# Identity products ahead of TensorE's waits in three layer norms and in the routing of a two-layer decoder trunk

## The chip, the cores and the metric

The kernel runs on one core of one Trainium2 chip. The metric is the device time of that core in microseconds (us), from one launch to its end. Several launches of the kernel before were timed, and one more was recorded by the hardware profiler.

## The reference

x has 256 tokens of 1024 channels, in float32. Two layers follow each other, each a mixer and a channel mixer, each followed by a residual layer norm:

```
layer 0:  x = LN(alpha*x + deltanet(x));   x = LN(alpha*x + swiglu(x))        # D_FF 2816
layer 1:  k, v = x @ w_kv
          x = LN(alpha*x + sliding_window_attention(x, k, v))
          x = LN(alpha*x + moe(x))                                            # 8 experts, 2 per token
moe(x):   logits = x @ w_router;  top_v, top_i = top_k(logits, 2)
          gates = one-hot sum of softmax(top_v)
          out = sum over e of gates[:, e] * ((silu(x @ g_e) * (x @ u_e)) @ d_e)
```

So there are four layer norms. The first three (after the DeltaNet mixer, after the dense SwiGLU, after the attention) are the inner ones; the last one ends the program and is not touched.

## The kernel before

**Products.** Every large product is made of three float32r products of a high and a low part (hi·hi, hi·lo, lo·hi). Weights arrive in units of 1 MB (two DMAs of 512 KB) in six `raw` slots; ScalarE cuts the high part (`cut_hi`, line 484), VectorE the rest (`cut_lo`, line 790), into three `hi`/`lo` slots. SyncE's queue issues the DMAs; each waits until VectorE has cut the unit that lay in its slot. TensorE waits for `lo_ready` of the unit it needs, uses it, and increments `unit_used`, on which ScalarE's next cut waits. Matmuls of all stages are issued by the helper `mm`, line 1226.

**Order of work.** Each engine has one hand-written program, and semaphores tie them together; nothing is reordered. On TensorE the inner norms look like this: `to_tokens` finishes the projection of the two token blocks of 128, block 0 first. VectorE's `norm` (lines 800 to 823) then works through block 0 and block 1: residual add out of PSUM (line 809), statistics (813, 815, 816), `x - mean` times gain (820), and, when POOL has raised the variance to the power -1/2 (line 374), the last step (823), which sets `ln_done`. TensorE's `turn_x` transposes the normed x in four steps `s` of four 128x128 blocks (line 1237), two steps per token block; before steps 0 and 2 it waits for `ln_done` of the block. ScalarE copies each step out of PSUM (`xT_hi`, line 490), VectorE takes the rest (`xT_lo`, line 798), and the first product of the next stage waits for these (`turn_lo`).

**Routing, after the third inner norm.** TensorE waits for the turned x (`turned_in(4)`), makes the logits by `small_product` (24 matmuls of 256 columns, line 1226), and signals `lg_mm`. VectorE cuts the low part of x for the gather (line 1100) and then copies the logits (line 1102, `lgT_here`); TensorE transposes them (line 1550); VectorE finds the two best experts in a chain of small operations and sets `sel_here` (line 1121); TensorE sums the selection with a triangular and an all-ones matrix (`pos_mm`), VectorE makes the gates, the positions and `cint` (lines 1124 to 1137, `route_here`), and the one-hot matrices (line 1148, `oneh_here`). TensorE then gathers the tokens of the first two experts with 32 matmuls of 256 columns (`gather`), turns the one-hots and picks the gates (`slots`), and waits for `xg_here`, that is until ScalarE (line 490) and VectorE (line 1156) have split the gathered tokens.

**Experts.** A hardware loop of four turns, two experts each, 33 weight units per expert: 22 for gate and up, 11 for down, 12 matmuls of 512 columns per unit. `experts(1)`, for more than 128 tokens on one expert, stands behind a condition.

In float32 (not float32r) one `mm` of 128x128 appears in the trace as two matmul instructions. `ident` is a float32 128x128 identity matrix that lies in SBUF from the start.

Of the kernel before, what the change touches and what calls it, by code (L numbers as in the profile page):

```python
# [25 lines left out]
P = 128  # L26
# [9 lines left out]
def trunk(nc, x_in, w_in, conv_w, a_log, dt_bias, norm_w, w_out, w_kv, w_q, sinks, w_o, w_gu, w_down,  # L36
          w_router, moe_gu, moe_down, ln_g, ln_b, out):
    _, T, D = x_in.shape
    NB = T // P
    KD = D // P  # L40
# [30 lines left out]
    with ctx:  # L71
        def sb(name, shape, dt=F32, where=None):
            return (where or ctx).enter_context(nc.sbuf_tensor(name, shape, dt))

        def sem(name):
            return ctx.enter_context(nc.semaphore(name))
# [5 lines left out]
        x = sb("x", [P, NB, D])  # L82
        lng = sb("lng", [P, D])
        lnb = sb("lnb", [P, D])
        ident = sb("ident", [P, P])
# [7 lines left out]
        ps = ctx.enter_context(nc.psum_tensor("ps", [P, 8, 512], F32))  # L93
# [104 lines left out]
        ln_var, ln_rstd, ln_done = sem("ln_var"), sem("ln_rstd"), [sem(f"ln_done{b}") for b in range(NB)]  # L198
# [1025 lines left out]
        def _(pe):  # L1224
            def mm(dst, lhsT, rhs, start, stop):
                return pe.matmul(dst, lhsT, rhs, start=start, stop=stop)  # L1226
# [4 lines left out]
            def turn(i, src, made=None):  # L1231

                for s in range(4):
                    if made is not None:
                        made(s)
                    for q in range(4):
                        last = pe.transpose(ps[:, 4 + s, q * P:(q + 1) * P], src(s // 2, 4 * (s % 2) + q), ident[:, :])  # L1237
                    last.then_inc(turned, 1)

            def turn_x(i, norms):  # L1240

                turn(i, lambda b, k: x[:, b, k * P:(k + 1) * P],
                     lambda s: pe.wait_ge(ln_done[s // 2], norms) if s % 2 == 0 else None)

            def turned_in(i):
                pe.wait_ge(turn_lo, 4 * i + 4)
# [56 lines left out]
            def small_product(dst, w_hi, w_lo):  # L1303

                for k in range(KD):
                    mm(dst, w_hi[:, k, :], xT_hi[:, k, :], k == 0, False)
                    mm(dst, w_hi[:, k, :], xT_lo[:, k, :], False, False)
                    last = mm(dst, w_lo[:, k, :], xT_hi[:, k, :], False, k == KD - 1)
                return last
# [142 lines left out]
            for u in range(2):  # L1452
                to_tokens([U_OUT + u], 2 * u, 2, u == 0, False, halves(0), xT_hi, xT_lo)
            to_tokens([U_OUT + 2, U_OUT + 3], 4, 2, False, True, halves(0), xT_hi, xT_lo, True)
            turn_x(2, 1)


            for c in range(FC):
                if c >= 3:
                    pe.wait_ge(ffn_act, c - 2)  # L1460
                for t in range(2):
                    bank = 2 * (c % 3) + t
# [6 lines left out]
            pe.wait_ge(ffn_lo, FC)  # L1469
            to_tokens([U_DOWN + FC - 2, U_DOWN + FC - 1], 2 * (FC - 2), 2, False, True, halves(4), hT_hi, hT_lo, True)  # L1470
            turn_x(3, 2)


# [66 lines left out]
            pe.wait_ge(pv_lo, HKV)  # L1540
            to_tokens([U_O + 2, U_O + 3], 4, 2, False, True, halves(0), oT_hi, oT_lo, True)
            turn_x(4, 3)

            turned_in(4)

            pe.wait_ge(wr_cut, 2)
            small_product(ps[0:E, 0, 0:T], wr_hi, wr_lo).then_inc(lg_mm, 1)
            pe.wait_ge(lgT_here, 1)
            for b in range(NB):
                last = pe.transpose(ps[:, 0, E * b:E * (b + 1)], lgT[:, b * P:(b + 1) * P], ident[0:E, 0:E])  # L1550
            last.then_inc(lg_mm, 1)
            pe.wait_ge(sel_here, 1)
            pe.wait_ge(consts, 3)
            mm(ps[:, 1, 0:E], tri_strict[:, :], sel[:, 0, :], True, True)
# [6 lines left out]
            def experts(p):  # L1561
                base = U_MOE + p * E * PER_E

                def gather(pair, it):

                    pe.wait_ge(oneh_here, 5 * p + pair + 1 + it)
                    for k in range(KD):
                        bank = 6 * (k // 4) + k % 4 // 2
                        dst = ps[:, bank, (k % 2) * 2 * P:(k % 2) * 2 * P + 2 * P]
                        c = slice(k * P, k * P + P)  # L1570
                        for n_, (part, b) in enumerate(((x3_hi, 0), (x3_hi, 1), (x3_lo, 0), (x3_lo, 1))):
                            last = mm(dst, part[:, b, c], oneh[:, b, :, :].rearrange("p e s -> p (e s)"), n_ == 0, n_ == 3)
                    last.then_inc(gathered, 1)

                def slots(ge, it, i):

                    for b in range(NB):
                        pe.transpose(ps[:, 4, b * P:(b + 1) * P], oneh[:, b, i, :].bitcast(F32), ident[:, :])
                    for b in range(NB):
                        last = mm(ps[:, 5, 0:1], oneh[:, b, i, :].bitcast(F32), gates[:, b, bass.ds(ge + 2 * it, 1)],  # L1580
                                  b == 0, b == 1)
                    last.then_inc(slots_mm, 1)
# [19 lines left out]
                        last.then_inc(scattered, 1)  # L1602

                if p == 0:
                    pe.wait_ge(route_here, 1)
                pe.wait_ge(x3_cut, 2)
                gather(0, 0)
                slots(0, 0, 0)
                pe.wait_ge(xg_here, 5 * p + 1)
                pe.wait_ge(moe_zero, 2 * p + 2)  # L1610
                with pe.Fori(0, TURNS) as it:
                    for b in range(2):
                        for l in range(PER_E):
                            j = base + PER_E * b + l
                            if l < 2 * FC:
# [9 lines left out]
                                for kk in range(4):  # L1625
                                    k = 4 * (l % 2) + kk
# [8 lines left out]
                            else:  # L1635
# [7 lines left out]
                                for kk in range(2):  # L1643
                                    k = 2 * d + kk
# [13 lines left out]
                scatter(E, 0, (E + 1) % 2)  # L1658

            experts(0)  # L1660
            full = pe.value_load(cint[0:1, 0:1], min_val=0, max_val=T)
            with pe.If(full > P):
                experts(1)
# [20 lines left out]
```

## Time and profile before

| | |
|---|---|
| timed runs | 1389.83, 1393.05, 1394.28 us (median 1393.05) |
| span of the profiled execution, its own time | 1389.1 us |
| TensorE, share of the span busy | 93% |
| VectorE | 75% |
| ScalarE | 60% |
| POOL | 6% |
| mean granted TensorE clock | 0.966 of full speed |
| HBM read | 351.5 MB |

The profiled execution is a launch of its own; its span runs from the first to the last instruction, and no other time of it is given. The median of the timed runs is 3.95 us above that span, the lowest of them 0.7 us. The granted clock is a share of 2.4 GHz: 1.00 in the rows is 2.4 GHz, 0.50 is 1.2 GHz. A timeline row gives start, duration, engine, line, operation and count, and in brackets how long the engine had been idle and what ended that.

### The profile page before, as it was taken

Reading aid. Unit: us, or ns where it says so; the run is one execution under the profiler, and the core shown is the slowest. Engines: PE = TensorE matmul, PEld = TensorE weight load, DVE = VectorE, ACT = ScalarE, POOL = GpSimd, SP = SyncE. Lnnn points to the kernel's source line nnn. Section 1 sums busy time; section 2 is a strip of 40 time slices with the busy share of each in tenths; the row PEclk is TensorE's granted clock in tenths of the full one; section 3 lists DMA queues with packets and bytes.
Section 4 is the critical chain, followed back from the end, with each engine's and each line's share of the span. In section 5 each row is a group of like instructions: output and inputs, shape, how many; then the busy total and the mean of one; then the engine's idle time right before and its main releaser. Section 6 shows DMA issues by size and latency. Waiting matters only on the chain.

```text
span 1389.1 us, 20039 instructions
## 1 busy us (share of the span) xinstructions
PE 1298.2 (93%) x7163; PEld 1118.7 (81%) x7163; DVE 1046.4 (75%) x947; ACT 840.0 (60%) x898; POOL 76.9 (6%) x100
## 2 busy tenths in 40 slices
PE   6998988999998977899999999999999998999993
PEld 5997986999987955788888788887888887888882
DVE  4876745444546576598897898997898987988977
ACT  4784342344433463477776777776777767777762
POOL 3034211000002001000000000000000000000000
PEclk9999998999998998799999999999999999999997
DMA  9643002555464332499998999998999998999991
GB/s 318 205 151 122 1 32 90 185 184 183 180 211 152 95 98 82 160 341 377 344 368 299 349 371 372 348 385 286 344 383 351 347 380 280 334 383 348 356 343 60
DMA packets 267406, 354.05 MB, mean 255 GB/s; under 512 B 11920, under 2 KB 236288, under 8 KB 267296
## 3 DMA queue, kind: packets, MB, share of 16 engines
q1 hardware_dynamic: 264832, 348.17, 74.1%
q0 software_dynamic: 1312, 4.31, 1.0%
q8 instruction: 68, 1.11, 0.3%
q14 instruction: 42, 0.34, 0.1%
q10 hardware_dynamic: 1152, 0.11, 0.1%
HBM read 351.50 MB, written 1.05 MB: 254 GB/s over the span
## 4 chain that ended last, share of the span: by engine, by line
PE 77%; DVE 12%; issue 5%; ACT 5%; POOL 1%; DMA 0%; DVEq 0%; POOLq 0%; ACTq 0%; SPq 0%
PE ps L1226 74%; DVE lo L790 5%; ACT hi L484 2%; PE ps L1589 1%; POOL lnrs L374 1%; DVE conv L852 1%; DVE xg_lo L1156 1%; DVE bnst L813 1%; DVE x L823 1%; PE ps L1237 1%; DVE x L809 1%; ACT sS L666 0%; DVE x L1173 0%; DMA x<-in_x 0%; DVE xT_lo L798 0%
## 5 line engine op out<-in xcount | busy, mean ns | idle before, releaser
L790 DVE TENSOR_TENSOR lo<-raw,hi 128x2048 fp32r<-128x2048 f32 x330 | 756.0, 2299 | 201.6 <-ACT hi L484 200.8
L484 ACT ACTIVATE hi<-raw 128x2048 fp32r<-128x2048 f32 x330 | 632.2, 1919 | 384.9 <-PE ps L1226 379.6
L1226 PE MATMUL ps<-hi,xg_hi 128*128 128x512 f32 x704 | 282.6, 401 | 10.9 <-issue 7.5
L1226 PE MATMUL ps<-hi,xg_lo 128*128 128x512 f32 x704 | 276.7, 393 | 0.0
L1226 PE MATMUL ps<-lo,xg_hi 128*128 128x512 f32 x704 | 275.9, 392 | 0.0
L1226 PE MATMUL ps<-xT_hi,hi 128*128 128x256 f32 x624 | 180.1, 289 | 1.3 <-DVE xT_lo L798 1.3
L1226 PE MATMUL ps<-xT_hi,lo 128*128 128x256 f32 x624 | 178.8, 287 | 0.0
L1226 PE MATMUL ps<-xT_lo,hi 128*128 128x256 f32 x624 | 178.8, 287 | 0.0
L1226 PEld LDWEIGHTS ps<-hi,xg_hi 128*128 128x128 f32 x704 | 133.3, 189 | 39.4 <-issue 12.2
L1226 PEld LDWEIGHTS ps<-hi,xg_lo 128*128 128x128 f32 x704 | 133.0, 189 | 28.7
L1226 PEld LDWEIGHTS ps<-lo,xg_hi 128*128 128x128 f32 x704 | 133.5, 190 | 25.9
L1226 PEld LDWEIGHTS ps<-xT_hi,hi 128*128 128x128 f32 x624 | 122.4, 196 | 2.2 <-issue 2.0
L1226 PEld LDWEIGHTS ps<-xT_lo,hi 128*128 128x128 f32 x624 | 122.3, 196 | 0.1
L1226 PEld LDWEIGHTS ps<-xT_hi,lo 128*128 128x128 f32 x624 | 122.1, 196 | 0.0
L1226 PE MATMUL ps<-hi,hE_hi 128*128 128x512 f32 x352 | 111.1, 397 | 2.6 <-DVE lo L790 2.6
L1226 PE MATMUL ps<-lo,hE_hi 128*128 128x512 f32 x352 | 108.7, 390 | 0.0
L1226 PE MATMUL ps<-hi,hE_lo 128*128 128x512 f32 x352 | 108.6, 390 | 0.0
L1226 PEld LDWEIGHTS ps<-lo,hE_hi 128*128 128x128 f32 x352 | 66.1, 188 | 14.1
L1226 PEld LDWEIGHTS ps<-hi,hE_lo 128*128 128x128 f32 x352 | 66.1, 188 | 14.1
L1226 PEld LDWEIGHTS ps<-hi,hE_hi 128*128 128x128 f32 x352 | 64.0, 188 | 16.0 <-DVE lo L790 4.2
L374 POOL TENSOR_TENSOR lnrs<-lnve,mhalf 128x1 f32<-128x1 f32 x8 | 12.2, 1524 | 1149.1 <-DVE lnve L816 1149.1
L852 DVE SCALAR_TENSOR_TENSOR conv<-ps,cw,conv 128x255 f32<-128x255 f32 (+2 forms) x72 | 29.2, 474 | 17.9 <-ACT conv L514 17.9
(275 smaller groups left out, 1397.1 us busy)
## 6 DMA issues: line engine op xcount, KB each, us to landing
raw<-in_moe_w_gu SPq DMA_DIRECT2D x358, 512.0 KB, 6.3
raw<-in_moe_w_down SPq DMA_DIRECT2D x176, 512.0 KB, 6.1
raw<-in_ffn_w_gu SPq DMA_DIRECT2D x44, 512.0 KB, 4.5
raw<-in_dn_w_in SPq DMA_DIRECT2D x32, 512.0 KB, 8.7
raw<-in_ffn_w_down SPq DMA_DIRECT2D x22, 512.0 KB, 4.2
raw<-in_dn_w_out SPq DMA_DIRECT2D x8, 512.0 KB, 3.9
raw<-in_sw_w_q SPq DMA_DIRECT2D x8, 512.0 KB, 4.0
raw<-in_sw_w_out SPq DMA_DIRECT2D x8, 512.0 KB, 4.5
```

The lines of the kernel that those rows point to most:

```text
L374: return pool.tensor_tensor(dst, src, mhalf[:, 0:src.shape[1]], ALU.pow)
L484: act.activation(slot(hi, j), slot(raw, j), ACT.Copy).then_inc(hi_ready, 1)
L790: dve.tensor_tensor(slot(lo, j), slot(raw, j), slot(hi, j).bitcast(F32), ALU.subtract).then_inc(lo_ready, 1)
L809: step(dve.scalar_tensor_tensor(out=x[:, b, :], in0=x[:, b, :], scalar=ALPHA, in1=ps[:, bank + 2 * b:bank + 2 * b + 2, :].rearrange("p b n ...
L813: link(dve.bn_stats(bnst[:, b, q, :], x[:, b, 512 * q:512 * q + 512]))
L823: dve.scalar_tensor_tensor(out=x[:, b, :], in0=x[:, b, :], scalar=lnrs[:, b:b + 1], in1=lnb[:, :], op0=ALU.mult, op1=ALU.add).then_inc(ln_ ...
L852: dve.scalar_tensor_tensor(out=conv[:, t, d:T], in0=ps[:, t % 4, 0:T - d], scalar=cw[:, w:w + 1], in1=conv[:, t, d:T], op0=ALU.mult, op1=A ...
L1156: last = dve.tensor_tensor(xg_lo[:, part, :, :].rearrange("p k e s -> p k (e s)"), ps[:, 6 * i:6 * i + 2, :].rearrange("p b (k s) -> p (b ...
L1226: return pe.matmul(dst, lhsT, rhs, start=start, stop=stop)
L1237: last = pe.transpose(ps[:, 4 + s, q * P:(q + 1) * P], src(s // 2, 4 * (s % 2) + q), ident[:, :])
L1589: last = pe.transpose(ps[:, 6 + gc % 2, m * P:(m + 1) * P], actE[:, gc % 2, m * P:(m + 1) * P], ident[:, :])
```

## The change

A helper `busy(n_, bank)` issues `n_` float32 products of the identity with itself into 128 columns of a PSUM bank. Nobody reads the result, and it signals nothing. It is called at six places of TensorE's program, each ahead of a wait that was there before: 18 products in each of the three inner norms, between the transposes of token block 0 and the wait for token block 1; and once each in the routing, 6 before the wait for the turned x, 3 before the logits' copy, 12 before the selection, 8 before the positions, 14 between `slots` and the wait for the split tokens. The other engines' programs are not touched, and no wait is added or removed.

```diff
+            def busy(n_, bank):
+                for _ in range(n_):
+                    mm(ps[:, bank, 0:P], ident[:, :], ident[:, :], True, True)
+
             def turn_x(i, norms):
 
-                turn(i, lambda b, k: x[:, b, k * P:(k + 1) * P],
-                     lambda s: pe.wait_ge(ln_done[s // 2], norms) if s % 2 == 0 else None)
+                def made(s):
+                    if s == 2:
+                        busy(18, 0)
+                    if s % 2 == 0:
+                        pe.wait_ge(ln_done[s // 2], norms)
+
+                turn(i, lambda b, k: x[:, b, k * P:(k + 1) * P], made)
...
             turn_x(4, 3)
 
+            busy(6, 3)
             turned_in(4)
 
             pe.wait_ge(wr_cut, 2)
             small_product(ps[0:E, 0, 0:T], wr_hi, wr_lo).then_inc(lg_mm, 1)
+            busy(3, 3)
             pe.wait_ge(lgT_here, 1)
...
             last.then_inc(lg_mm, 1)
+            busy(12, 3)
             pe.wait_ge(sel_here, 1)
...
                 if p == 0:
+                    busy(8, 3)
                     pe.wait_ge(route_here, 1)
                 pe.wait_ge(x3_cut, 2)
                 gather(0, 0)
                 slots(0, 0, 0)
+                if p == 0:
+                    busy(14, 3)
                 pe.wait_ge(xg_here, 5 * p + 1)
```

## Rows read from the trace of the kernel before

**Rows 1.** The page's clock row, the span in 40 equal slices, in tenths.
```profile
PEclk9999998999998998799999999999999999999997
```

**Rows 2.** TensorE's waits over the span: us in total, times, longest us.
```profile
PE ps L1237 <- DVE x L823: 16.2, 6, 4.8
...
PE ps L1226 <- DVE xg_lo L1156: 3.3, 1, 3.3
PE ps L1226 <- DVE sel L1121: 2.8, 1, 2.8
```

**Rows 3.** Timeline at the first inner norm: start us, us, engine, line, operation.
```profile
230.67 0.61 PE L1226 MATMUL ps<-hi,xT_lo 128*128 128x512 f32 x2
...
231.90 1.09 PE L1237 MATMUL ps<-ident,x 128*128 128x128 f32 x8 [0.62 <-DVE x L823]
...
237.78 1.97 PE L1237 MATMUL ps<-ident,x 128*128 128x128 f32 x8 [4.78 <-DVE x L823]
...
240.40 0.55 PE L1226 MATMUL ps<-xT_hi,hi 128*128 128x256 f32 x1 [0.65 <-DVE xT_lo L798]
...
245.65 0.41 PE L1226 MATMUL ps<-xT_hi,hi 128*128 128x256 f32 x1
...
246.29 0.34 PE L1226 MATMUL ps<-xT_hi,hi 128*128 128x256 f32 x1
...
246.59 0.28 PE L1226 MATMUL ps<-xT_hi,lo 128*128 128x256 f32 x1
...
247.30 0.28 PE L1226 MATMUL ps<-xT_hi,lo 128*128 128x256 f32 x1
```

**Rows 4.** Stretches: length, busy us by engine, clock, DMA share, GB/s.
```profile
233.00:236.00 3.00, 0.00 (x0) 0.00 (x0) 2.84 (x5) 1.26 (x3) 1.19 (x1) 1.00 0.00 0
...
439.00:444.20 5.20, 5.20 (x24) 5.20 (x25) 5.18 (x3) 0.00 (x0) 4.57 (x6) 0.50 0.67 224
...
550.30:553.50 3.20, 0.89 (x8) 0.43 (x5) 1.91 (x10) 1.07 (x1) 0.00 (x0) 1.00 0.00 0
...
558.70:563.70 5.00, 5.00 (x24) 5.00 (x24) 4.21 (x2) 0.00 (x0) 0.00 (x0) 0.50 0.31 78
...
568.90:574.00 5.10, 5.10 (x12) 4.04 (x13) 0.00 (x0) 0.00 (x0) 0.00 (x0) 0.50 0.00 0
574.20:580.00 5.80, 5.80 (x27) 4.78 (x26) 3.23 (x2) 4.79 (x3) 0.00 (x0) 1.00 0.04 7
```

**Rows 5.** Chain that ended last, in the routing and at an expert: start us, us, what.
```profile
542.70 1.98 PE ps L1237 x8
...
546.08 4.83 PE ps L1226 x24
...
550.93 0.42 DVE lgT L1102
...
554.51 2.32 PE ps L1226 x10
...
558.65 6.37 PE ps L1226 x32
...
601.93 5.50 PE ps L1226 x24
```

**Rows 6.** Timeline: float32 products of 128x128, and the routing's small products of one column.
```profile
178.62 1.06 PE L1226 MATMUL ps<-Nm,Dm 128*128 128x128 f32 x8
179.51 1.06 PE L1226 MATMUL ps<-conv,Tm 128*128 128x128 f32 x8
...
565.06 0.50 PE L1226 MATMUL ps<-gates,oneh 128*128 128x1 f32 x4
```

**Rows 7.** Timeline: VectorE in the routing.
```profile
547.13 2.29 DVE L1100 TENSOR_TENSOR x_lo<-x,x_hi 128x2048 fp32r<-128x2048 f32 x1 [1.10 <-ACT x_hi L490]
...
556.93 0.17 DVE L1133 SCALAR_TENSOR_TENSOR lg<-ps,sel 128x16 f32<-128x16 f32 x1 [0.65 <-PE ps L1226]
```

**Rows 8.** A stretch of the attention, columns as in the stretches above.
```profile
488.80:492.10 3.30, 1.75 (x12) 1.28 (x12) 3.30 (x10) 2.28 (x4) 0.00 (x0) 1.00 0.05 17
```

## The prediction, written before the run

> **What bounds the kernel now.** I read the page first: TensorE is busy 93% of the span, and its granted clock is full in most slices but dented in a few [rows 1]. A dent costs time only where TensorE sets the pace, so I looked at its waits. The six waits for a normed block add up to 16.2 us, the longest 4.8; the routing adds single waits of 2.8 us (selection) and 3.3 us (split tokens) [rows 2]. No product can be moved into these waits: each is a chain through VectorE, ScalarE and POOL. What follows them is what I priced.
>
> The timeline of the first inner norm shows it. The projection ends at about 231.3; TensorE idles until the second block is normed, 4.78 us up to 237.78 [rows 3]. The clock is 1.00 up to 236 although the engine has stood still since 233 [rows 4], and low after that: the eight transposes of block 0 took 1.09 us, those of block 1 take 1.97 [rows 3]. It is still low when the SwiGLU starts at 240.40: three matmuls of 256 columns take 0.64 us there (245.65 to 246.29), 0.213 us each, and six take 0.71 us from 246.59 on, 0.118 each [rows 3]. So TensorE, which has no further wait there, pays 1.2 GHz for about 28 matmuls (240.40 to 246.3).
>
> The stretches show the same pattern four times more [rows 4]: after the second norm (24 matmuls at 0.50), in the gather (24 of its 32), and in the first expert unit (12 matmuls of 512 columns in 5.10 us, then 1.00); the logits' 24 matmuls take 4.83 us, 0.20 each [rows 5], after the third norm. In each case the clock had fallen in the wait ahead, and rose only after some microseconds of work without a gap.
>
> **What the change costs.** It adds 97 products: 3 x 18, then 6, 3, 12, 8, 14. Price of one: eight float32 instructions of 128x128, four products, start at 178.62 and the next eight at 179.51 [rows 6], so 0.223 us a product at full clock. At 1.2 GHz I double it less the small overhead, 0.427 us (twice the 0.213 of the 256-column matmul, which streams as many cycles). Against the waits, at full clock:
> - 18 products take 4.0 us in a wait of 4.78 us, three times.
> - 6 take 1.3 us before the turned x; the wait there is 1.4 us (544.68 to 546.08 [rows 5]) and grows to some 1.7 when the transposes ahead of it run at full clock.
> - 3 take 0.7 us before the logits' copy, which itself takes 0.42 [rows 5] and, as shown below, starts late; 0 to 0.2 us of overshoot.
> - 12 take 2.7 us in 2.8, 14 take 3.1 in 3.3 [rows 2]; 8 take 1.8 in 1.8 (556.83 to 558.65 [rows 5]), or 2.3 once the sums ahead run at full clock.
>
> So the fills cost nothing while the clock is up: they end just before the wait does, TensorE's queue holds only work that needs the waited-for data, and nothing else waits on TensorE in these stretches (the cuts of the next weight units wait on products issued before). The cover is thin, 0.1 to 0.8 us a site. At 1.2 GHz it is gone; that is the price of the slower rival below.
>
> **What it gives, site by site,** if the clock stays at 1.00:
> 1. Norm 1. The eight transposes of block 1 take 1.97 us cold and 1.09 at full clock [rows 3], so the first four end about 0.5 us sooner, and ScalarE's copy, VectorE's rest and the first product all follow: 0.5 us. Then 28 matmuls x (0.213 - 0.118) = 2.6 us. Sum 3.1 us.
> 2. Norm 2, same code: 0.5 + 25 x 0.095 = 2.9 us. Nothing takes it back before the attention: TensorE is without a gap there [rows 4].
> 3. Norm 3 and logits. The turned x comes about 0.65 us sooner and some 20 of the 24 matmuls are cold, 1.9 us: TensorE would be 2.5 us early. But VectorE must first make the low part of x, 2.29 us from 547.13 [rows 7], behind ScalarE's copies, which move up by only 0.7 us or so. It ends at 548.7, and the logits' copy starts then and not at 550.93 [rows 5]: 2.2 us. What is late next is VectorE.
> 4. Selection sums. 10 small float32 instructions take 2.32 us [rows 5]; four of one column took 0.50 us at full clock [rows 6], so ten take about 1.2. VectorE stands idle for 0.65 us before it uses the sums [rows 7], so only 0.6 us of the 1.1 counts.
> 5. Gather: 24 x 0.095 = 2.2 us. VectorE's two cuts beside it (4.21 us busy [rows 4]) end before ScalarE's first copy of gathered tokens, so they don't hold it.
> 6. First expert unit: 12 x (0.425 - 0.229) = 2.4 us, with 0.425 from 5.10 us for 12 [rows 4] and 0.229 from 24 matmuls in 5.50 us [rows 5]. Three units lie cut and six raw ones are loaded (DMA share 0.00 [rows 4]), so the earlier start moves the cuts and the DMAs with it.
>
> The sum is 3.1 + 2.9 + 2.2 + 0.6 + 2.2 + 2.4 = 13.4 us against the span of 1389.1 us, that is 1375.7. The median of the runs is 3.95 us above this span. When the clock recovers differs from execution to execution (cold times of 5 to 6 us after the norms here), so I take 13 us off the median: **1380 us**. The two unknown costs are bounded thus: the overshoot of six fills is 0 us at full clock and up to 10 us at half (below); the hold of the clock is worth nothing (the rows' falls all repeat) up to the full 13.4 us. I take the full-clock ends, for two reasons. First, in 488.80 to 492.10 TensorE was busy 1.75 of 3.30 us with transposes alone and the clock stayed at 1.00 [rows 8]; in 550.30 to 553.50 it was busy 0.89 us of 3.20, and it fell after that [rows 4]: the ten small instructions that follow take 2.32 us [rows 5]. With the fills the emptiest part of a norm runs from the last identity products over the eight transposes to the first matmul, 3 us with 1 us of work: between those two, and the stretches around it are full. Second, the operands are mostly zeros, but so are the gather's one-hot matrices, and the clock rose during the gather: its first 24 matmuls take some 5.1 us, the last eight the remaining 1.2 [rows 4, 5].
>
> A rule speaks against this. The Trainium skill, "TensorE: Matmul & The Clock Gate", Part 4 on the transpose, says that transposes don't count as TensorE being busy in the same way, and its closing table wants no idle gap over about 3 us between bursts. By that rule the 2.9 us or so from the fills' end to the next product would be nearly one gap, and the clock might fall just as the product starts. The transposes of rows 8 speak against it; no row shows transposes ahead of such a product after a fill.
>
> **Rivals.**
> - *The clock falls in what is left of the wait* (0.8 us, transposes, 1.1 us). Then sites 1 and 2 keep the 0.5 us each and lose the 5.0 us, and site 3 loses 1 to 2 us. The rest, 6 to 7 us, remains: 1386.5 us. For it: the eight transposes of block 0 did not hold it over the wait that follows [rows 3]. Against: [rows 8]. That rule of the skill is this rival. Chance 0.13.
> - *What the experts' start gains is given back.* VectorE is the second busiest engine, a cut takes it about as long as the 2.29 us of [rows 7], and a warm unit takes TensorE 2.7, so cuts may lag behind a faster first unit: 11 us remain, 1382 us. Against: the third cut starts when the first unit is used, and that distance stays the same. Chance 0.12.
> - *Slower: identity products don't hold the clock.* It falls where it falls now, inside the fills, and the rest of each runs at 0.427 us. With a fall at 236, 3.0 of the 4.0 us run at full clock and the rest doubles, 5.0 against 4.78 us; with a fall a little sooner up to 0.8 over; I take 0.4 a norm, 1.2 us; 6 products cold cost 2.6 against 1.4, with later transposes 1.9 us over; 3 cost 0.8, 12 cost 2.3, 8 cost 1.6, 14 cost up to 2.7 us over. Sum 10.5 us: 1403 us. The point from which it decides is whether the clock is 0.50 when the 12, the 8 and the 14 run. For it: the operands are an identity, of which no row shows a whole product. Chance 0.05.
> - *The change does nothing to the clock and the fills hide*, or gains and overshoots cancel: 1393 us. Chance 0.04.
>
> The forecast itself has 0.66.
>
> **How the numbers follow.** Runs of before lie 4.5 us apart, so I call 0.3%, 4.2 us, what a measurement can tell from no change. Forecast, first and second rival are all faster by more than that: 0.66 + 0.13 + 0.12 = 0.91; same 0.04; slower 0.05. The range takes in the first two rivals and 4 us below the forecast for the spread of the runs: 1376 to 1387 us. Outside it lie the last two rivals and the tails, together below 0.2.
>
> **What would show it.** Right: the clock 1.00 from the projection before each inner norm to the stage behind it; the SwiGLU's first matmuls 0.118 us apart; the logits, gather and first expert unit at full clock; TensorE's waits at the six places shorter, 0.1 to 0.8 us each; the logits' copy starting as VectorE's line 1100 ends; first expert matmul about 11 us earlier in the span. Wrong: a clock of 0.50 in a stretch with identity products, a fill that ends after the semaphore it precedes was set, or an experts' stage that takes longer than before by what was won ahead of it.

## The result, and the profile after

The changed kernel took 1381.92 us (median of four runs, 1378.51 to 1383.47), the kernel before on the same chip 1391.44 us (four runs, 1389.11 to 1394.28): ratio 0.9926, interval 0.9905 to 0.9947. That is faster by more than 0.3%, 1.9 us above the forecast of 1380 and inside the range of 1376 to 1387. Two more comparisons of the same code gave 0.9932 and 0.9923 (below). One execution of a_again (1424.36 us, granted clock 0.885) and one of transposes (2189.63 us, 0.559) were slow, and no median here has them in it.

| | before | after |
|---|---|---|
| span of the profiled execution | 1389.1 us | 1380.7 us |
| mean granted clock | 0.966 | 0.981 |
| first expert matmul starts | 568.89 us | 558.59 us |
| first expert matmul to TensorE's last one ("the loop" below) | 801.3 us | 802.8 us |

The page's clock row of the changed kernel, 40 slices:

```profile
PEclk8999999999999989999999999999999999999997
```

The dents of [rows 1] at the norms and in the routing are gone; the one that stays in the middle (slice 15) is in the attention, and the 8 in slice 1 belongs to the program's start, where the clock was at half for 10.2 us (6.8 before). TensorE's waits after the change (us in total, times, longest), to be set beside [rows 2]:

```profile
PE ps L1226 <- issue: 18.2, 5, 7.2
...
PE ps L1237 <- DVE x L823: 4.2, 6, 0.8
...
PE ps L1226 <- DVE oneh L1148: 0.4, 1, 0.4
```

The six waits for a normed block fell from 16.2 to 4.2 us, the longest from 4.8 to 0.8; those for the selection (2.8) and the split tokens (3.3) no longer appear. What remains at the one-hots is 0.4 us. The timeline at the first inner norm, to be set beside [rows 3]:

```profile
232.96 4.18 PE L1226 MATMUL ps<-ident 128*128 128x128 f32 x36
237.90 1.09 PE L1237 MATMUL ps<-ident,x 128*128 128x128 f32 x8 [0.76 <-DVE x L823]
...
240.06 0.36 PE L1226 MATMUL ps<-xT_hi,hi 128*128 128x256 f32 x1 [1.07 <-DVE xT_lo L798]
...
240.25 0.28 PE L1226 MATMUL ps<-xT_lo,hi 128*128 128x256 f32 x1
...
240.61 0.28 PE L1226 MATMUL ps<-xT_lo,hi 128*128 128x256 f32 x1
```

Eighteen products are 36 instructions and take 4.18 us; TensorE then still waits 0.76 us, so they delay nothing. In the routing some fills leave no wait that the list shows, but what follows isn't late either: TensorE starts 0.05 us after VectorE's line 1121 and 0.43 us after line 1156, in both kernels. The second eight transposes take 1.09 us and not 1.97. The SwiGLU's first matmuls follow each other about every 0.12 us (240.25 to 240.61 is three), where they took 0.213 before. The stretches (columns as in [rows 4]) of the stages behind the fills, in order: norm 1, norm 2, logits, gather, first two expert units; the sixth stage, the selection sums, reads 1.00 too.

```profile
240.10:246.00 5.90, 5.90 (x49) 5.90 (x50) 4.81 (x3) 0.00 (x0) 1.76 (x8) 1.00 0.93 283
...
435.60:441.00 5.40, 5.40 (x45) 5.40 (x46) 4.79 (x3) 0.00 (x0) 4.75 (x7) 1.00 0.87 247
...
540.40:543.40 3.00, 3.00 (x27) 2.40 (x28) 2.06 (x1) 0.90 (x1) 0.81 (x1) 1.00 0.82 268
...
550.70:554.60 3.90, 3.90 (x33) 3.90 (x34) 3.90 (x2) 0.00 (x0) 0.00 (x0) 1.00 0.12 16
...
558.60:564.10 5.50, 5.50 (x24) 4.58 (x25) 0.52 (x1) 1.92 (x1) 0.00 (x0) 1.00 0.41 139
```

All read 1.00. In 5.5 us TensorE now does 24 expert matmuls, two units; before, 5.1 us held 12 [rows 4]. The chain that ended last (start us, us, what), beside [rows 5]:

```profile
541.34 2.29 DVE x_lo L1100
...
543.63 0.33 DVE lgT L1102
...
550.64 4.06 PE ps L1226 x32
...
558.59 8.45 PE ps L1226 x36
```

The logits' copy (line 1102) starts at 543.63, the moment VectorE's line 1100 ends: VectorE sets the pace there now, as the prediction said. The gather takes 4.06 us, not 6.37.

Measured as distances between the starts of the same instructions in the two timelines, the stages came out so:

| step of the prediction | predicted | measured, us |
|---|---|---|
| 1. norm 1 and SwiGLU's start | 3.1 | 3.1 (8.50 to 8.03, and 190.08 to 187.45) |
| 2. norm 2 and what follows, up to norm 3 | 2.9 | 2.0 in this profile, 3.2 and 4.8 in the two others of the changed kernel (below) |
| 3. norm 3 to the logits' copy | 2.2 | 2.4 (14.11 to 11.69) |
| 4. selection sums | 0.6 | 0.6 (4.14 to 3.52) |
| 5. gather | 2.2 | 2.3 (10.24 to 7.95) |
| 6. first expert unit | 2.4 | 2.45 (first two units, 8.02 to 5.57) |
| everything after these two units | 0 | +3.9 (793.3 to 797.2) |

### The profile page after: what moved, and what is told of

Its sections match the earlier page's. It is cut to its first block, busy times and chain, and to the rows that moved or that the text cites. A ratio compares the mean times of both kernels' runs of the same rounds, so it can differ in the third digit from the quotient of the medians.

```text
span 1380.7 us, 20427 instructions
## 1 busy us (share of the span) xinstructions
PE 1307.3 (95%) x7357; PEld 1130.1 (82%) x7357; DVE 1045.7 (76%) x947; ACT 839.8 (61%) x898; POOL 76.8 (6%) x100
## 4 chain that ended last, share of the span: by engine, by line
PE 76%; DVE 12%; issue 5%; ACT 5%; POOL 1%; DMA 0%; DVEq 0%; POOLq 0%; ACTq 0%; SPq 0%
PE ps L1226 74%; DVE lo L790 6%; ACT hi L484 2%; PE ps L1601 1%; POOL lnrs L374 1%; DVE conv L852 1%; DVE bnst L813 1%; DVE x L823 1%; DVE xg_lo L1156 1%; DVE x L809 1%; ACT sS L666 1%; DVE x L1173 1%; DMA x<-in_x 0%; DVE xT_lo L798 0%; PE ps L1237 0%
## 5 line engine op out<-in xcount | busy, mean ns | idle before, releaser
L1226 PEld LDWEIGHTS ps<-hi,xg_hi 128*128 128x128 f32 x704 | 133.4, 190 | 37.5 <-issue 10.3
```

## The experiments

Two questions were open. Is the gain the clock, held by work of any kind ahead of a wait, or something else? And where did the last row's 3.9 us go? Each diff is against the changed kernel unless said otherwise. Ratios are to the kernel before, run in the same comparison; its median there was 1390.71 us (a_again, norms_only, routing_only, transposes), 1391.1 us (before_b, norm6, norm36, turn8) and 1391.85 us (a_third, transposes_b, norm36_shift, attn14).

### The same code again (a_again, a_third)

No edit. These two show by how much two executions of one code differ.

> The changed kernel once more, same code. Compared stage by stage, the two traces on hand give the six stages of the change 13.6 us, and take about 4 us back at the turns of the expert loop (three falls of the clock there instead of one, some 1.6 us each, and one longer gap) and 0.8 us in the attention. Theory L (luck of when the clock looks): the falls at the turns are unrelated to the fills; this profile shows another number of them, from 0 to 3, and the median of these runs lies 8 to 13 us below the kernel before. Theory S (systematic): the fills or the earlier start make the loop slower; again three falls at the turns, 9 to 10 us below.

> The changed kernel a third time, beside the others on the same chip: 8.5 to 10.5 us faster than before, 1 to 3 falls of the clock at the turns of the expert loop, 801 to 803 us from first to last expert matmul.

Measured: a_again 1380.51 us, 0.9932 (0.9909 to 0.9955); a_third 1380.77 us, 0.9923 (0.9907 to 0.9940). The stages of steps 1 and 3 to 6 repeat within 0.03 us. Two things don't. From the first product behind the second norm to the third norm's transposes it took 96.31, 95.08 and 93.51 us in the three profiles (the changed kernel's first, a_again, a_third), with the clock at half for 10.2, 6.8 and 3.4 us after the attention's 3.8-us wait (before: 97.85, with 6.8). And the expert loop varies with its turns.

The loop is some 798 us and the falls of the clock in it. At the three inner turns TensorE waits 1.5 to 3.4 us, and at some of them the granted clock goes to 0.50 for 3.4 us; in the three profiles of the changed kernel a turn with a fall takes 200.4 to 201.1 us, one without 198.9 to 199.4, so a fall costs about 1.6 us. Stretches at three turns of the changed kernel:

```profile
757.30:760.50 3.20, 3.02 (x7) 2.45 (x8) 2.54 (x2) 1.72 (x2) 0.00 (x0) 0.50 1.10 349
...
958.70:961.90 3.20, 3.20 (x9) 2.46 (x8) 1.67 (x1) 0.65 (x1) 0.00 (x0) 0.50 1.12 352
...
1160.00:1163.30 3.30, 3.30 (x9) 2.59 (x8) 1.47 (x1) 0.44 (x1) 0.00 (x0) 0.50 1.10 350
```

and at the third of the kernel before, the only one of its three with a fall:

```profile
1168.10:1171.30 3.20, 3.20 (x9) 2.52 (x8) 1.35 (x1) 0.33 (x1) 0.00 (x0) 0.50 1.10 349
```

Three falls after the change, one before: 3.2 us, most of the 3.9. The first of the waits was also 1.2 us shorter before (1.48 against 2.69). But a_again had two falls and its loop took 801.7 us; a_third had three and took 802.8.

### The kernel before again (before_b)

No edit, the kernel before.

> The kernel before once more, for a second profile of its expert loop. The first showed a cold first unit (2.4 us), one fall at a turn and one short wait (1.5 us in place of 2.9), 801.3 us from first to last expert matmul. Theory L (luck): another number of falls at the turns, 802 to 804 us. Theory S (the cold first unit protects the turns): 801.3 again, at most one fall at a turn.

Measured: 1392.52 us in one run, span 1390.8, loop 803.6 us, with two falls:

```profile
771.10:774.30 3.20, 3.20 (x9) 2.41 (x9) 0.67 (x1) 0.00 (x0) 0.00 (x0) 0.50 1.10 349
...
1170.50:1173.70 3.20, 3.20 (x9) 2.46 (x9) 1.48 (x1) 0.66 (x2) 0.00 (x0) 0.50 1.10 349
```

So the number of falls changes from execution to execution in either kernel. Over all profiles, those whose first unit ran at half clock for all or part of it had one, two and one falls at the turns (before, before_b, norms_only); the nine others with a loop of the usual length had two or three. The first profile of before was a lucky one by some 1.6 us; whether a warm start makes a fall likelier too stays open. The profile also settles a smaller point: reported time and span differ by 1.7 to 1.9 us in every run on record (1392.52 less 1390.8 here), so the first profiled execution stood for about 1390.8 us, not 1393.05.

### Each half alone (norms_only, routing_only)

The first diff is norms_only, the second routing_only.

```diff
-            busy(6, 3)
...
-            busy(3, 3)
...
-            busy(12, 3)
...
-                    busy(8, 3)
...
-                if p == 0:
-                    busy(14, 3)
```

```diff
-                    if s == 2:
-                        busy(18, 0)
```

> Only the 18 products in the three inner norms; no fills in the routing. Terms of the prediction: norm 1 3.1, norm 2 2.9, norm 3 and logits 2.2 us if the clock is still up when the logits are made without the 6 products (the wait before them is 1.7 us), then the clock falls in the selection wait as before and the gather and the first expert unit are cold. Expected 8 us faster than before (6 to 9). If the norms' fills do nothing for the clock: 0 us or slower.

> Only the fills of the routing (6, 3, 12, 8, 14), not those of the norms. The clock is at 1.2 GHz when the 6 products run (2.6 us against a wait of 1.4), so the logits start about 1.2 us late and run cold until the clock rises; from then on it is held: selection sums 0.6, gather 2.2, first expert unit 2.4. Expected 3 to 5 us faster than before. If a fill at half clock never lifts it, the 12, 8 and 14 all overshoot: 6 to 8 us slower.

Measured: norms_only 1382.6 us, 0.9945 (0.9926 to 0.9965), 8.1 us less than its neighbour before; routing_only 1387.49 us, 0.9974 (0.9962 to 0.9986), 3.2 us less. Together 11.3, against 10.2 for the whole in the same comparison: the two halves add up. Each shortens its own stages. In norms_only the norms and the logits take what they take in the changed kernel, the selection sums 4.14 us as before, the gather 9.94 (10.24 before, 7.95 changed), the first two units 7.18 (8.02 and 5.57); in routing_only everything is as before up to the third norm, and the sums, the gather and the first units are as in the changed kernel. One fill turns out to be idle: norms_only has no six products ahead of the logits, and its logits' copy comes as early (11.69 us after the third norm's first transposes), because VectorE sets the pace there.

routing_only shows the other regime, in which the clock had fallen before the fill. Its stretches over the fill and the logits, and two lines of its timeline:

```profile
540.50:547.10 6.60, 3.96 (x19) 3.97 (x20) 4.78 (x7) 2.55 (x3) 4.16 (x5) 0.50 0.32 110
...
547.30:550.00 2.70, 2.70 (x26) 2.08 (x26) 2.29 (x1) 0.34 (x2) 0.00 (x0) 1.00 0.28 99
```

```profile
544.90 2.62 PE L1226 MATMUL ps<-ident 128*128 128x128 f32 x12
...
547.28 0.36 PE L1226 MATMUL ps<-xT_hi,wr_hi 128*8 128x256 f32 x1
```

Six products at 0.50 take 2.62 us, 0.44 each (the prediction's 0.427), and the logits start 0.8 us later after the transposes than before (4.15 against 3.38 us). Yet the clock is 1.00 as they start, and the stage is 1.1 us shorter all the same (13.03 against 14.11). The slower rival's prices are real, but here the overshoot was paid back by an earlier rise of the clock.

### Transposes as the fill (transposes, transposes_b)

```diff
-                    mm(ps[:, bank, 0:P], ident[:, :], ident[:, :], True, True)
+                    for _ in range(2):
+                        pe.transpose(ps[:, bank, 0:P], ident[:, :], ident[:, :])
```

> Each of the 97 products is replaced by two transposes of the identity, which take as long (0.117 us each at full clock, 0.23 a pair). If transposes hold the clock as products do: same time as the changed kernel, within 2 us, clock 1.00 in all stages. If transposes don't count, as the rule of the skill has it: the clock falls where it fell before, inside the fills, the rest of each fill runs at half speed, and the kernel is 5 to 10 us slower than before, 15 us slower than the changed one.

> The kernel with transposes in place of products once more; its median was 3.2 us below the changed kernel's, though the six stages took the same time to 0.02 us. If that was luck in where the clock fell elsewhere: within 2 us of the changed kernel in this comparison. If transposes are better: again 3 us faster.

Measured: 1378.20 us, 0.9904 (0.9882 to 0.9926), and 1379.07 us, 0.9911 (0.9898 to 0.9924). The timeline and the stretches at the first norm:

```profile
232.23 4.09 PE L1243 MATMUL ps<-ident 128*128 128x128 f32 x36
...
237.17 1.09 PE L1237 MATMUL ps<-ident,x 128*128 128x128 f32 x8 [0.85 <-DVE x L823]
```

```profile
232.30:236.30 4.00, 4.00 (x37) 3.78 (x35) 3.38 (x7) 1.36 (x3) 1.53 (x1) 1.00 0.00 0
...
236.40:239.30 2.90, 1.09 (x8) 0.86 (x8) 2.72 (x5) 1.08 (x2) 1.54 (x4) 1.00 0.09 16
```

Thirty-six transposes fill 4.09 us, the clock stays 1.00 over them and over the 2.9 us behind them, which hold 1.09 us of transposes, and steps 1 and 3 to 6 are those of the changed kernel within 0.05 us (the stretch with the attention in it took 93.51 and 95.08 us, as in a_third and a_again). This was the rule weighed in the prediction, that transposes don't count as TensorE being busy in the same way (the Trainium skill, "TensorE: Matmul & The Clock Gate", Part 4). Here a fill of transposes alone holds the clock as well as one of products. The medians are 2.3 and 1.7 us below the products' in the same comparisons. The stages don't show why, the intervals overlap, and it stays open.

### Fills too short and too long (norm6, norm36, norm36_shift)

The diff is that of norm6; norm36 and norm36_shift have `busy(36, 0)` there, and norm36_shift has the second edit too.

```diff
-                        busy(18, 0)
+                        busy(6, 0)
```

```diff
+            busy(14, 3)
             attend(1)
```

> 6 products in each norm in place of 18, 1.3 us, so that some 3.5 us of the wait stand empty before the second block's transposes. If the clock follows how much TensorE does, it falls again in most norms: sites 1 and 2 lose 2.6 us each and site 3 part of its 2.4, the kernel is 4 to 7 us slower than the changed one. If any work at all in the wait is enough: same time as the changed kernel.

> The fills of the three norms doubled, 36 products in place of 18. At 0.223 us a product 18 more take 4.0 us, and only 0.8 us of wait is left, so each norm should overshoot by 3.2 to 3.3 us: 9.7 us slower than the changed kernel, about the time of the kernel before. If a product costs less than 0.223 us or more of the wait is left: less.

> The kernel with doubled norm fills (1408 us) plus 14 more products in the attention, in front of a wait of 3.8 us, so that by themselves they cost nothing. Its expert loop took 820.0 us instead of 802: TensorE stopped for 4.3 to 4.9 us after the third matmul of turns 2, 3 and 4. Theory A (the place of the loop's first instruction in the 16 KB blocks in which instructions arrive decides): 14 products are 56 more instructions ahead of the loop, which move its start past the block's end, and the second stop goes: 801 to 804 us for the loop, some 17 us faster than the kernel with doubled fills, about the time of before. Theory B (a later or longer program as such, or a late weight transfer): the stops stay, 818 to 822 us for the loop.

norm6 took 1385.79 us, 0.9954 (0.9934 to 0.9974), 5.3 us less than the kernel before, where the changed kernel won 9.5 to 11.1. Its timeline at the first norm:

```profile
232.68 1.50 PE L1226 MATMUL ps<-ident 128*128 128x128 f32 x12
...
237.62 1.09 PE L1237 MATMUL ps<-ident,x 128*128 128x128 f32 x8 [3.44 <-DVE x L823]
...
240.56 0.41 PE L1226 MATMUL ps<-xT_hi,hi 128*128 128x256 f32 x1
...
241.20 0.41 PE L1226 MATMUL ps<-xT_hi,hi 128*128 128x256 f32 x1
```

Six products leave 3.44 us idle. The transposes still run at full clock, but the first matmuls don't (three in 0.64 us from 240.56): the fall comes later and costs 2.5 us up to the second norm (189.94 us, not 187.45). A fill has to cover most of its wait.

norm36 took 1408.44 us, 1.0126 (1.0108 to 1.0145): 17 us slower than the kernel before, far from what either theory expected. Two of its places, in the timeline:

```profile
233.43 8.20 PE L1226 MATMUL ps<-ident 128*128 128x128 f32 x72
...
243.58 0.36 PE L1226 MATMUL ps<-xT_hi,hi 128*128 128x256 f32 x1 [1.07 <-DVE xT_lo L798]
...
765.91 0.79 PE L1226 MATMUL ps<-hi,xg_hi 128*128 128x512 f32 x1 [2.67 <-issue]
766.50 0.63 PE L1226 MATMUL ps<-lo,xg_hi 128*128 128x512 f32 x1
766.92 0.63 PE L1226 MATMUL ps<-hi,xg_lo 128*128 128x512 f32 x1
...
771.96 0.80 PE L1226 MATMUL ps<-hi,xg_hi 128*128 128x512 f32 x1 [4.41 <-issue]
```

The first lines are the expected overshoot: the fill runs past the wait, and the norm takes 11.07 us and not 8.03, 3.04 us more, three times. Those 9.1 us are a third of the some 27 us by which it is above the changed kernel. The rest is in the loop, 820.0 us: from its second turn on TensorE stops again after the third matmul, 4.41, 4.87 and 4.28 us, with "issue" as the cause. Nothing in the loop had been edited; its code had only moved in the program. norm36_shift tests that: 56 more instructions ahead of the loop. It took 1389.92 us, 0.9985 (0.9972 to 0.9998), its loop 802.6 us, and the same place reads:

```profile
764.43 0.79 PE L1226 MATMUL ps<-hi,xg_hi 128*128 128x512 f32 x1 [2.55 <-DVE lo L790]
...
765.45 0.63 PE L1226 MATMUL ps<-hi,xg_lo 128*128 128x512 f32 x1
765.87 0.63 PE L1226 MATMUL ps<-hi,xg_hi 128*128 128x512 f32 x1
```

The fourth matmul follows 0.42 us after the third. (The profile names a cut of VectorE for the 2.55 us, but that cut had ended 0.98 us before TensorE went on.) So the place of the loop's start in the program cost 17.4 us, and more instructions made the kernel 18.5 us faster. It isn't the program's length either: norm36 has 216 matmuls and weight loads more ahead of the loop than the changed kernel. The other kernels here stand at seven other distances, from 388 fewer (before) to 272 more (norm36_shift), and none of them has the second stop.

What TensorE waits for can be read from the instruction queue's packets (q8, some 16 KB each) in narrow windows of the DMA view. norm36, 769.2 to 770.5 us (packets, MB, share):

```profile
q8 instruction: 1, 0.02, 5.2%
```

It is the only one between the stop's start at 767.6 and its end at 771.96. In all three such stops TensorE goes on 2.5 to 2.7 us after the start of such a packet, and at every one of the three inner turns, in all fourteen profiles, 2.7 to 3.0 us after one. In norm36_shift the same second packet runs too (767.9 us), but TensorE doesn't run out of instructions before it has come. So both kinds of stop are waits for instructions. The number of packets over the whole span says nothing: 70 in norm36 and 67 in norm36_shift, but 68 and 69 in before and norm6, which have no second stop.

### A fill at the loop's turn (turn8)

The line stands last in the body of the hardware loop, behind the second expert's `slots`, and runs once a turn.

```diff
+                    busy(8, 0)
```

> The changed kernel, and 8 more identity products at the end of each turn of the expert loop, ahead of the wait of some 2.9 us in which the clock fell 1 to 3 times in every profile so far. If those falls are what takes back part of the gain: no fall at a turn, from the first to the last matmul of the experts 797 to 799 us (801.7 and 802.8 in the two profiles of the changed kernel), and the kernel some 3 us faster than the changed one, 12 to 13 us faster than before. If the wait is TensorE fetching the loop's instructions, so that the fill isn't hidden: 1.8 us longer a turn, 5 to 7 us slower than the changed kernel.

Measured: 1394.8 us, 1.0031 (1.0014 to 1.0049), 3.7 us slower than the kernel before and so 13 to 15 us slower than the changed one; the loop took 815.7 us. The timeline at the first turn, of the changed kernel and then of turn8:

```profile
754.83 1.11 ACT L760 ACTIVATE y_hi<-ps,gslot 128x1024 fp32r<-128x1024 f32 x1 [0.80 <-PE ps L1226]
...
757.48 0.79 PE L1226 MATMUL ps<-hi,xg_hi 128*128 128x512 f32 x1 [2.69 <-issue]
```

```profile
754.48 1.95 PE L1226 MATMUL ps<-ident 128*128 128x128 f32 x16
...
761.11 0.79 PE L1226 MATMUL ps<-hi,xg_hi 128*128 128x512 f32 x1 [4.68 <-issue]
```

At the turn no data is late: TensorE waits for its own instructions. In the changed kernel it resumes 2.7 us after its last product, in turn8 4.68 us after a fill of 1.95 us: 3.9 us more at this turn, 3.4 to 3.9 at the three. The fill didn't hide. The packets show why not: in the changed kernel the turn's instruction packet starts at 754.6, as TensorE's last matmul ends (754.79), in turn8 at 758.2, and each time TensorE goes on 2.8 to 2.9 us later. So the fetch begins only behind the fill. That it begins 1.7 us after the fill's end, in all three turns, is more than the fill's length explains, and it stays open. The half-clock stretch behind each turn is 6.8 us here and not 3.4.

The Trainium skill, "Runtime: NRT & Kernel Launch", section "Instruction fetch mechanics", says that a taken branch whose target isn't at hand forces a DMA fetch before the engine goes on; the turns agree, at 1.5 to 3.4 us each. It calls the crossing from one 16 KiB block to the next mostly hidden; norm36 is a case where it isn't, if its second stop is that crossing. That the stop ends with the next packet and goes away with a shift fits; the blocks' borders themselves are in no trace.

### A fill in the attention (attn14)

```diff
+            busy(14, 3)
             attend(1)
```

> The changed kernel plus the same 14 products (3.1 us) in front of the attention's wait of 3.8 us, where the clock fell in every profile. From the fourth stage's first matmul to the third norm's transposes 93 to 94 us instead of 95.1 and 96.3; 1.5 to 2.5 us faster than the changed kernel, if the loop keeps its 802 us. If the fill is too late to hold the clock: same as the changed kernel.

Measured: 1381.2 us, 0.9926 (0.9911 to 0.9942), no different from the changed kernel. The fill went to the wrong wait. Timelines of attn14, then of the changed kernel (a_third):

```profile
480.82 3.29 PE L1226 MATMUL ps<-ident 128*128 128x128 f32 x28
...
493.35 2.58 PE L1511 MATMUL ps<-ident,sS 128*128 128x128 f32 x12 [2.15 <-DVE sS L1066]
```

```profile
483.66 1.09 PE L1511 MATMUL ps<-ident,sS 128*128 128x128 f32 x8 [1.27 <-DVE sS L1066]
...
494.74 2.88 PE L1511 MATMUL ps<-ident,sS 128*128 128x128 f32 x12 [3.78 <-DVE sS L1066]
```

It stands ahead of the 1.3-us wait and delays TensorE there; the later wait, the one after which the clock falls, shrinks to 2.15 us, and the clock fell all the same (6.8 us at half). The stretch took what a_again took (95.05 against 95.08 us). So it doesn't tell whether a fill at the 3.8-us wait would save the fall; that stays open.

## Why the prediction was right, and where it was off

**What bounds the kernel: right.** In the six stages TensorE's half clock was what made them long, and where another engine takes over once it is full (VectorE at the logits' copy, and in the selection sums), the prediction had counted only the part that is left. norms_only and routing_only each bring their own part.

**The fills' cost: right.** 36 instructions take 4.18 us (4.0 predicted), and no fill held back what followed it; the covers were thinner than predicted in the routing, where three of the five fills end together with their waits. The prices at half clock were right too (0.44 a product in routing_only), though this changes no sum, since the clock never fell in a fill of the changed kernel.

**The six gains: right.** Five steps came within 0.25 us. Step 2 gave 3.2 us in a_again, which has the same 6.8 us at half clock in the attention as the kernel before, against 2.9. In the first profile 1.2 us of it was lost to the longer fall there; in a_third a shorter one brought 1.6 more. The size of this step is luck by some 3 us, since it follows a fall that the change doesn't touch. The first expert matmul came 10.3 us sooner (predicted about 11).

**"The sum is the gain": this step failed.** The prediction let everything behind the first expert unit take what it took before. The loop took 3.9 us more there in the first pair of profiles, and 0.6 us more between before_b and a_again (795.6 and 796.2 behind the first two units). The mechanism was not the rival's: VectorE's cuts didn't hold the units (TensorE's waits for them, line 790, are 2.6 us in all in both kernels). In the first pair it was the clock's falls at the loop's turns (3.2 of the 3.9 us), which the prediction never priced, though the kernel before has one at 1168.1. The measured gains (9.5, 10.2 and 11.1 us) are 2 to 4 us below the 13.4 of the sum. Two or three falls against one or two account for a part of that, some 1.6 us if it is one more on average; the 11.8 us that are left lie within all three intervals. Whether the change brings the additional fall or chance does, no run decides.

**The basis: off by 2 us.** The forecast took 13 us off 1393.05. The execution that was read stood for 1390.8 us. The two errors cancel in part: 13.4 us off 1390.8 would have been 1377.4, below all three medians of the changed kernel. That the forecast came within 2 us is therefore partly luck; by its own steps it would have been 4.5 us too low, still inside the range.

**The rivals.** That the clock falls in the rest of the wait is excluded at 18 products and comes true at 6 (norm6). That identity products don't hold the clock is excluded. The give-back rival named the right size, 1382 us, and the wrong mechanism.

## What to carry to other kernels

Where TensorE waits some microseconds on another engine and is itself the bound of the next stage, unread products of about the wait's length, ending a little before it does, keep the clock up: here 97 of them bring 9.5 to 11 us of 1391. Measure the length from both sides, since too few lose a stage's gain and too many go straight onto the path, and don't put them ahead of a loop's branch, where the wait is for instructions and, here, began only after them. After any edit ahead of a hardware loop, compare the loop's own time, for its place in the program can cost more than the edit.

## What had not been expected of the hardware

- A turn of the hardware loop stops TensorE for 1.5 to 3.4 us, until 2.7 to 3.0 us after the start of a 16 KB instruction packet, and the clock may fall behind it, in one to three of the three inner turns of an execution, at about 1.6 us each.
- Moving the unedited loop in the program brought stops of 4.3 to 4.9 us after the third matmul of a turn, each ended by a further such packet; 56 instructions more ahead of it took them away (820.0 and 802.6 us).
- A fill of nothing but identity transposes holds the granted clock at 1.00 in all six stages.
